# A sliding-window attention block and a second attention block on one core: three reorderings around the attention units

## The reference, cut to what matters

```python
def first_block(x, ...):            # 32 heads of 64, 4 heads of keys and values
    return x + swa_sink_mixer(rms_norm(x, swa_norm), ...)

def swa_sink_mixer(h, w_in, q_gain, k_gain, sinks, rel_table, w_out):
    q, k, v, gate = split(h @ w_in)
    q, k = rms_norm(q, q_gain), rms_norm(k, k_gain)      # per head
    bias = rel_table[t5_bucket(max(dist, 0))]            # per head, 128 x 256
    for each block j of 128 queries:
        s = q_j @ k[two blocks].T * scale + bias         # outside the band: -inf
        m = max(max(s), sink)
        p = exp(s - m); p = p / (sum(p) + exp(sink - m))
        o_j = p @ v[two blocks]
    return (o * silu(gate)) @ w_out
```

## Time and profile before

| | |
|---|---|
| median of 3 runs | 2002.7 us (2002.26 to 2003.86) |
| the profiled execution's own time | 2000.68 us |
| its span | 1999.0 us |
| TensorE (PE) busy | 1909.8 us, 96% |
| VectorE (DVE) / ScalarE (ACT) busy | 917.6 us, 46% / 849.0 us, 42% |
| DMA | 173.47 MB, mean 87 GB/s |
| mean granted clock of TensorE | 0.985 |

### The profile page before, as it was taken

One profiled execution on the slowest core, in us unless ns is written; L12 is line 12 of the kernel. 1 busy time (PEld: TensorE's weight loads), 2 busy tenths in 40 slices (PEclk: granted clock), 3 DMA queues, 4 the chain that ended last, 5 costly groups with the idle time before them and its releaser, 6 DMA issues.

```text
span 1999.0 us, 28285 instructions
## 1 busy us (share of the span) xinstructions
PE 1909.8 (96%) x9973; PEld 1552.3 (78%) x9973; DVE 917.6 (46%) x2224; ACT 849.0 (42%) x1946; POOL 35.3 (2%) x64
## 2 busy tenths in 40 slices
PE   6899999999998999999999999999999999989999
PEld 5677777777776888888888787888878888766887
DVE  4355455555556333544445434454444445444221
ACT  4355555555555323434435343342433435244221
POOL 1000000000000000000000000000000000000000
PEclk9899999999998999999999999999999999998999
DMA  7822222222213444422222222222222222204452
GB/s 190 197 69 74 69 74 69 74 69 75 74 54 101 135 131 132 112 80 74 68 74 68 71 64 75 73 71 77 56 74 73 76 63 75 64 11 121 139 140 84
DMA packets 299827, 173.47 MB, mean 87 GB/s; under 512 B 22880, under 2 KB 289696, under 8 KB 299744
## 3 DMA queue, kind: packets, MB, share of 16 engines
q1 hardware_dynamic: 294368, 157.55, 28.2%
q0 software_dynamic: 4304, 13.98, 2.7%
q10 hardware_dynamic: 1088, 1.08, 0.3%
HBM read 156.86 MB, written 14.66 MB: 86 GB/s over the span
## 4 chain that ended last, share of the span: by engine, by line
PE 91%; ACT 4%; DMA 2%; DVE 1%; issue 1%; SPq 0%; ACTq 0%; DVEq 0%
PE G L465 72%; PE S L751 2%; DMA raw<-in_swa_w_in 2%; ACT p L1006 2%; PE G L586 2%; PE O L586 1%; PE O L824 1%; PE S L796 1%; PE O L768 1%; ACT p L996 1%; PE T L742 1%; PE S L563 1%; PE S L813 1%; PE G L573 1%; PE S L562 1%
## 5 line engine op out<-in xcount | busy, mean ns | idle before, releaser
L465 PE MATMUL G<-xh,wh 128*128 128x512 f32 (+1 forms) x2624 | 894.9, 373 | 4.9 <-DVE xl L1523 4.9
L465 PE MATMUL G<-xl,wh 128*128 128x512 f32 (+1 forms) x2624 | 846.3, 354 | 0.0
L465 PE MATMUL G<-xh,wl 128*128 128x512 f32 (+1 forms) x2624 | 842.5, 353 | 0.0
L465 PEld LDWEIGHTS G<-xh,wh 128*128 128x128 f32 x2624 | 466.6, 190 | 103.8 <-issue 37.3
L465 PEld LDWEIGHTS G<-xh,wl 128*128 128x128 f32 x2624 | 462.8, 190 | 70.5
L1336 DVE TENSOR_TENSOR wl<-raw,wh 128x512 fp32r<-128x512 f32 x528 | 353.4, 687 | 354.1 <-ACT wh L901 352.9
L465 PEld LDWEIGHTS G<-xl,wh 128*128 128x128 f32 x2624 | 462.6, 189 | 62.0 <-issue 3.4
L901 ACT ACTIVATE wh<-raw 128x512 fp32r<-128x512 f32 x528 | 314.2, 619 | 131.2 <-PE G L465 108.0
L1213 ACT ACTIVATE att<-att,st 128x144 f32<-128x144 f32 (+3 forms) x64 | 36.9, 577 | 184.7 <-DVE wmeta L1708 103.4
L996 ACT ACTIVATE p<-S,rq 128x256 f32<-128x256 f32 (+1 forms) x128 | 50.2, 444 | 105.8 <-PE S L563 105.8
L586 PE MATMUL O<-pT,v 128*128 128x256 f32 x96 | 29.3, 414 | 42.7 <-ACT pT L1015 42.7
(11 more groups left out here) (230 smaller groups left out, 1678.9 us busy)
## 6 DMA issues: line engine op xcount, KB each, us to landing
raw<-in_w_in SPq DMA_DIRECT2D x112, 512.0 KB, 4.0
raw<-in_swa_w_in SPq DMA_DIRECT2D x72, 512.0 KB, 3.7
raw<-in_swa_w_out SPq DMA_DIRECT2D x32, 512.0 KB, 5.1
raw<-in_w_out SPq DMA_DIRECT2D x32, 512.0 KB, 4.7
raw<-in_w_in POOLq DMA_DIRECT2D x8, 1024.0 KB, 7.9
rel_rows<-relb SPq DMA_DIRECT2D x1, 6128.0 KB, 35.8
mixed<-in_x SPq DMA_DIRECT2D x4, 1024.0 KB, 8.8
bias<-rel_rows POOLq DMA_DIRECT2D x16, 256.0 KB, 3.2
```

Source lines behind the costliest of these rows:

```text
L465: mm = pe.matmul(d, w[:, slot, k, :], v[:, k, a:b], start=(k == 0 and n == 0), stop=(k == KC - 1 and n == 2))
```

## The change

Three things change:

1. In each step of a unit ScalarE copies the transposed probabilities (`swa_pT`) before it evicts scores and takes exponentials.
2. The write of `rel_rows` moves from SyncE's queue to GpSimd's; ScalarE's eviction of the scores of unit 0 waits for its end, because the buffer of the probabilities lies over `relb`.
3. `first_factors` moves from p = 1 to p = 3 of the tile g = 1, and the steps of the chain of keys and values move two points later or so: TensorE p = 3, 4 to p = 5, 6; ScalarE m = 1, 4, 6 to m = 4, 6, 7 (the last now behind the split of m = 6); VectorE m = 0, 5 to m = 3, 7.

```diff
@@ sync
-            sp.wait_ge(rel_ok, 1)
-            sp.dma_start(bass.AP(tensor=rel_rows.tensor, offset=0,
-                                 ap=[[P * REL_PITCH, HEADS], [REL_PITCH + 1, P], [1, REL_COLS]]),
-                         relb[:, :].rearrange("h (a n) -> h a n", a=1).broadcast_to([HEADS, P, REL_COLS])).then_inc(rel_out, 16)
@@ gpsimd
+            pool.wait_ge(rel_ok, 1)
+            pool.dma_start(bass.AP(tensor=rel_rows.tensor, offset=0,
+                                   ap=[[P * REL_PITCH, HEADS], [REL_PITCH + 1, P], [1, REL_COLS]]),
+                           relb[:, :].rearrange("h (a n) -> h a n", a=1).broadcast_to([HEADS, P, REL_COLS])).then_inc(rel_out, 16)
             pool.wait_ge(rel_out, 16)
             bias_rows(0, 0)
@@ tensor, tiles of keys and values
-                    if g == 1 and p == 1:
+                    if g == 1 and p == 3:
                         first_factors()
-                    if g and p == 3:
+                    if g and p == 5:
                         kv_stat_of(g - 1)
-                    if g and p == 4:
+                    if g and p == 6:
                         kv_transpose(g - 1)
@@ tensor, query tile of unit 0
-                    elif p in (3, 4):
-                        (kv_stat_of if p == 3 else kv_transpose)(KV - 1)
+                    elif p in (5, 6):
+                        (kv_stat_of if p == 5 else kv_transpose)(KV - 1)
@@ scalar, tiles of keys and values (and the same in the query tile of unit 0)
-                    if m == 1:
+                    if m == 4:
                         kv_chain(g - 1)
-                    if m == 4:
+                    if m == 6:
                         kv_rstd(g - 1)
-                    if m == 6:
-                        kv_split(g - 1)
                     if m % 2 == 0:
                         split((g + 1) // 2, (g + 1) % 2, m // 2, kv_loaded(g + 1))
+                    if m == 7:
+                        kv_split(g - 1)
@@ scalar, swa_evict
                 after(act, q_rs, u + 1)
+                if isinstance(u, int) and u == 0:
+                    act.wait_ge(rel_out, 16)
@@ scalar, swa_step
+                if m in SWA_T:
+                    swa_pT(u, SWA_T[m])
                 if m in SWA_S:
                     swa_evict(u, SWA_S[m])
                 if m - 2 in SWA_S:
                     swa_exp(u, g, SWA_S[m - 2])
-                if m in SWA_T:
-                    swa_pT(u, SWA_T[m])
@@ vector, tiles of keys and values (and the same in the query tile of unit 0)
-                    if m == 0:
+                    if m == 3:
                         kv_evict(g - 1)
-                    if m == 5:
+                    if m == 7:
                         kv_finish(g - 1)
-                    if m == 7:
                         kv_split(g - 1)
```

More of the change, by code:

```diff
@@ L1049, in swa_window @@
                         swa_step(u - 1, window(i, g)[1], 8 + m)
-                    elif m == 1:
+                    elif m == 4:
                         kv_chain(KV - 1)
-                    elif m == 4:
+                    elif m == 6:
                         kv_rstd(KV - 1)
-                    elif m == 6:
+                    elif m == 7:
                         kv_split(KV - 1)
@@ L1498, in swa_window @@
                         swa_step(ip, u - 1, gp, 8 + m)
-                    elif m == 0:
+                    elif m == 3:
                         kv_evict(KV - 1)
-                    elif m == 5:
+                    elif m == 7:
                         kv_finish(KV - 1)
-                    elif m == 7:
                         kv_split(KV - 1)
```

## The result

The changed kernel takes 1947.88 us (median; 1947.02 to 1949.3), the one before 2002.48 in the same comparison: a ratio of 0.9732, 95% interval 0.9715 to 0.9749, or 54.6 us less. The forecast was 1941, 61.4 us less, with a range of 1935 to 1951. So the sign and the range held, 7 us are missing, and the narrower forecast of 1936 to 1946, which had 0.62, was missed. The profiled execution has a span of 1945.5 us (1999.0 before).

What follows compares the result with a forecast made beforehand. TensorE, busy 96% of the span, was taken to bound the kernel. Savings of 43.7 + 10.7 + 7.0 = 61.4 us took the profiled 2000.68 to 1939.3; the median lies 2.0 above, so 1941 us, range 1935 to 1951.

Steps and rivals of the forecast that it cites:

- Part 1: Copying transposed probabilities first removes both TensorE waits for them in each of fifteen units, 42.2 us, plus 1.5: 43.7 us.
- T(1): TensorE's transposing of block 1's scaled probabilities in a unit: reached at 4.06 us, with 0.1 us slack, the smallest.
- V(0): A unit's first value product on TensorE: at 2.14 us after its start instead of 3.45, finding its copy done.
- T(3): TensorE's last transposing step in a unit: reached at 12.85 us, after its scaling ends near 12.1.
- The 1.5 us for the last unit: Last unit, nothing between steps: later V(2) and T(3) come about 1.5 us earlier, bounds 0 and 2.5.
- Part 3: Moving factors and chain later removes the 2.9 us factor wait and keeps the clock up from 41 us: 7.0 us.
- the new wait at `kv_stat`: TensorE's first key statistics, only four chunks behind the factors, wait for the square: 0.5 us, bounds 0 and 1.5.
- Part 2: Table on GpSimd's queue: unit 0's query weights arrive in time, the 8.03 us TensorE wait and low clock go: 10.7 us.
- some 5.4 to one, about equal bytes: Weight packets per table packet when queues share engines, read from bias reads beside weights; a 512 KB load takes 5 us.
- the signs named for part 2: No ScalarE wait for unit 0's weights, no 0.50 clock near 80, table landing before 93, no wait at ScalarE's first eviction.
- the table starves the weights: Rival, chance 0.17: one weight packet per two-row table packet, 18 us a load, second half landing at 82, 1949 us.
- The table's own deadline: Table lands near 88 us, between 80 and 93; ScalarE's first eviction needs it at 94.7; costs zero, up to 4.

Runs made afterwards that it cites:

- act_evict_first: From act_queue, with the order within a step changed to swa_evict, then swa_pT, then swa_exp: 1948.59 us.
- pt_only: The kernel before, with only swa_pT put ahead of swa_evict and swa_exp in ScalarE's step: 1956.4 us.
- act_queue: The changed kernel with the table's write issued on ScalarE's hardware queue instead of GpSimd's, in single-row packets of 1.5 KB: 1939.64 us.
- act_factors: From act_queue, all points put back as in the kernel before, except first_factors at p = 3: 1943.22 us.
- half_factors: The changed kernel with 16 of 32 heads' tables written, first_factors at p = 3 and the chain at its old points: 1954.38 us.

## Why the prediction was right, and where a step failed

**Part 1** held step by step in the fifteen units: both waits gone, no new one, T(1) the tightest place (act_evict_first shows that 0.26 us there cost their full size). The term was 43.7 and measured 45.7. The units brought 44.7 instead of 42.2, since T(1) follows V(0) after 1.82 us, not after the 1.92 that I had carried over, and T(3) is at 12.71, not at 12.85. The 1.5 us for the last unit are not in the traces: 14.5 us before, 14.3 in the changed kernel, 13.9 in pt_only.

**Part 3** forecast 7.0, is 5.4 where it shows and 3.3 when it stands alone. The factors' wait and the low clock went as forecast; the new wait at `kv_stat` that I put at 0.5 is 0.3 (the last large matmul starts at 47.24, `kv_stat` at 47.74, 0.23 of it the usual spacing). The size is off because the low clock, 10.2 us long in the row I used, lasts 6.8 us in the other executions. At half the clock that is 5.1 us lost against 3.4, and these 1.7 us are about the difference between 7.0 and 5.4.

**Part 2** is the step that failed, and it is this sentence: "some 5.4 to one, about equal bytes". From rows in which bias reads and weights overlapped for 2 us I took a ratio of packets and built the load's 5 us on it. Once both queues moved, the ratio was within 2% of 1.00 in each of the stretches above, and the load took 25 us of turns, 32.9 from issue to landing with the pause before them. So two of the signs named for part 2 failed: ScalarE waited 15.14 us for unit 0's weights, and the clock was 0.50 from 85 to 90 us. The rival "the table starves the weights" had this very rule, put the second half's landing at 82 (it was 84.4) and the time at 1949 (measured 1947.9), and got 0.17. Its number is partly luck: it counted on packets of two rows, on 18 us for each half and on no pause, where the first half took 6.8 us and the second 32.9. The Trainium skill's sentence on the turns (DMA: Bandwidth & Descriptors, Queues, rings and completion order) was the better guide; the trace agrees with it: 205 to 205, 616 to 620. The trace of the kernel before already had the right ratio. Read in quarters of a microsecond, the 2 us of the earlier trace rows are a mixture: where the bias reads flow (here 86.00 to 86.25 and 87.50 to 87.75) it is near one for one, and between the two reads (86.75 to 87.00) their queue is nearly empty:

```profile
q0 software_dynamic: 16, 0.06, 76.8%
q1 hardware_dynamic: 21, 0.01, 17.9%
...
q0 software_dynamic: 19, 0.08, 95.8%
q1 hardware_dynamic: 14, 0.01, 11.1%
...
q1 hardware_dynamic: 139, 0.07, 104.4%
q0 software_dynamic: 6, 0.00, 6.3%
```

The sum also treated the parts as additive. Alone they bring 45.7, 0.4 and 3.3, together 54.6: parts 2 and 3 end on one event, the landing of unit 0's weights, and a gain in front of it is lost unless the landing moves too. The table's own deadline, on which I spent more words, was never near: it landed at 84.2 (forecast 88), and ScalarE's first eviction, at 104.2, did not wait.

## What to carry to other kernels

A long background transfer should have small packets: another queue alone does not protect the urgent loads beside it, since the turns go by packets, not by bytes (with table packets of 4.6 KB a load of 512 KB took 25 us of turns, with 1.5 KB about 8). A ratio of two queues must be read where both are full, not over a window in which one of them starts and ends. Price two edits that end on the same wait together, by asking what that wait waits for after both. And where an in-order engine serves several chains, put the short copy that the bottleneck waits for first, and compute the new slack of every later step; a tenth of a microsecond matters if it recurs, and no table of waits shows it.

## What was not expected of the hardware

- A load issued behind a running table of another queue moved no packet for about 8 us (issued at 51.52 in the changed kernel; 24 packets by 60), and only then took its turns. Beside the single-row packets it was some 5 us (act_queue: the loads ahead were through by 48.5, and the first half moved from about 53.5). Its cause stays open.
- The rate of the table depends on where it is read: 32 adjacent partitions 6128 KB in 38.7 us, the first 16 of them 3064 KB in 35.0, 16 spread over 32 the same bytes in 20.9.
- The clock fell after a stop of 1.90 us in act_factors and did not after the same stop in half_factors, nor in the units before the change with two stops of 1.14 and 1.35 us each. Once low behind these waits, it stayed so for 6.8 us in five of the profiled executions and for 10.2 in one.
